# Order and size of the first weight loads, of the first two chunks' passes, and of ScalarE's splits ahead of three feed-forward stages

## What is computed

```
x += 0.5 * SwiGLU_1(rms(x))
x += Mixer_l(rms(x))        # layer 0: gated DeltaNet + short conv; layer 1: sliding-window attention
x += 0.5 * SwiGLU_2(rms(x)) # and a final RMSNorm after layer 1
SwiGLU(h) = (silu(h @ w_gate) * (h @ w_up)) @ w_down     # 1024 -> 2816 -> 1024
```

## Time and profile before

| | us |
|---|---|
| median of 3 executions | 996.03 (995.19 to 999.85) |
| profiled execution | 996.98 |
| its span, first to last instruction | 995.0 |
| TensorE busy in it | 978.2 |
| VectorE busy | 622.2 |
| ScalarE busy | 475.8 |

### The profile page before, as it was taken

The page is one execution under the profiler, slowest core; times in us unless marked ns, Lnnn a source line. Parts: engine busy times, 40 slices in busy tenths (PEclk is TensorE's granted clock), DMA queues, the critical chain, the costliest instruction groups (busy, mean ns, idle before and its releaser), DMA issues.

```text
span 995.0 us, 19436 instructions
## 1 busy us (share of the span) xinstructions
PE 978.2 (98%) x8172; PEld 959.3 (96%) x8172; DVE 622.2 (63%) x619; ACT 475.8 (48%) x527; POOL 78.4 (8%) x76
## 2 busy tenths in 40 slices
PE   8999999999999999999999999999999999999997
PEld 8999999999999999999999999999999998999996
DVE  6755555799955566555557655555789486555554
ACT  7644444656543454343436534343647365343443
POOL 0100101000000011010100110101002101000000
PEclk9999999999999999999999999999999999999999
DMA  9665656453433356656555565566551254656551
GB/s 293 223 230 183 206 174 211 130 172 122 135 120 96 117 170 214 209 174 206 183 197 170 177 203 186 194 195 216 165 174 48 81 184 158 225 191 193 190 190 42
DMA packets 136309, 172.84 MB, mean 174 GB/s; under 512 B 4309, under 2 KB 123850, under 8 KB 136266
## 3 DMA queue, kind: packets, MB, share of 16 engines
q1 hardware_dynamic: 135792, 171.63, 53.4%
q10 hardware_dynamic: 474, 0.58, 0.2%
HBM read 171.15 MB, written 1.05 MB: 173 GB/s over the span
## 4 chain that ended last, share of the span: by engine, by line
PE 90%; DVE 4%; ACT 2%; issue 2%; DMA 1%; POOL 0%; SPq 0%; POOLq 0%; ACTq 0%; DVEq 0%
PE bank L363 24%; PE bank L368 24%; PE bank L364 24%; PE bank L714 6%; PE bank L1525 3%; DVE w_lo L334 1%; DMA raw<-in_ffn_w_up 1%; ACT w_hi L322 1%; PE bank L954 1%; PE bank L941 1%; PE bank L1585 1%; DVE var L528 1%; PE bank L930 0%; POOL silu_r L691 0%; PE bank L1601 0%
## 5 line engine op out<-in xcount | busy, mean ns | idle before, releaser
L334 DVE TENSOR_TENSOR w_lo<-raw,w_hi 128x2048 fp32r<-128x2048 f32 x152 | 349.8, 2301 | 188.1 <-ACT w_hi L322 188.0
L363 PE MATMUL bank<-h_hi_rest,w_hi 128*128 128x256 f32 x1428 | 393.7, 278 | 0.7 <-DVE h_lo_rest L486 0.6
L364 PE MATMUL bank<-h_lo_rest,w_hi 128*128 128x256 f32 x1428 | 392.4, 277 | 0.0
L368 PE MATMUL bank<-h_hi_rest,w_lo 128*128 128x256 f32 x1428 | 385.0, 277 | 0.0
L322 ACT ACTIVATE w_hi<-raw 128x2048 fp32r<-128x2048 f32 x159 | 302.8, 1908 | 140.3 <-PE bank L368 138.5
L363 PEld LDWEIGHTS bank<-h_hi_rest,w_hi 128*128 128x128 f32 x1428 | 268.2, 188 | 1.4 <-DVE h_lo_rest L486 0.8
L364 PEld LDWEIGHTS bank<-h_lo_rest,w_hi 128*128 128x128 f32 x1428 | 268.2, 188 | 0.0
L368 PEld LDWEIGHTS bank<-h_hi_rest,w_lo 128*128 128x128 f32 x1428 | 263.9, 188 | 0.0
L363 PE MATMUL bank<-act_hi,w_hi 128*128 128x256 f32 x480 | 133.6, 278 | 3.8 <-DVE w_lo L334 3.8
L364 PE MATMUL bank<-act_lo,w_hi 128*128 128x256 f32 x480 | 133.4, 278 | 0.0
L368 PE MATMUL bank<-act_hi,w_lo 128*128 128x256 f32 x480 | 133.3, 278 | 0.0
(11 more groups left out here) (285 smaller groups left out, 1240.7 us busy)
## 6 DMA issues: line engine op xcount, KB each, us to landing
raw<-in_ffn_w_up SPq DMA_DIRECT2D x44, 1024.0 KB, 5.3
raw<-in_ffn_w_down SPq DMA_DIRECT2D x44, 1024.0 KB, 4.9
raw<-in_ffn_w_gate SPq DMA_DIRECT2D x43, 1024.0 KB, 5.3
raw<-in_hyb_w_in SPq DMA_DIRECT2D x14, 1024.0 KB, 5.4
raw<-in_swa_w_qkv SPq DMA_DIRECT2D x6, 1024.0 KB, 5.1
raw<-in_hyb_w_out SPq DMA_DIRECT2D x4, 1024.0 KB, 5.3
raw<-in_swa_w_o SPq DMA_DIRECT2D x4, 1024.0 KB, 5.1
raw<-in_ffn_w_gate SPq DMA_DIRECT2D x2, 512.0 KB, 6.9
```

The source lines that it names most:

```text
L334: nc.vector.tensor_tensor(w_lo[slot(ch)][:], raw[:, slot(ch), :], w_hi[slot(ch)][:].bitcast(F32), ALU.subtract).then_inc(lo_split, 1)
L363: nc.tensor.matmul(out_ap, w_hi[s][:, wcols], mv_hi, start=start, stop=False, skip_group_check=True)
L364: i = nc.tensor.matmul(out_ap, w_hi[s][:, wcols], mv_lo, start=False, stop=False, skip_group_check=True)
L368: return nc.tensor.matmul(out_ap, w_lo[s][:, wcols], mv_hi, start=False, stop=stop, skip_group_check=True)
```

## The change

Four edits. (1) The first chunk's weights come in DMAs of 256, 256 and 512 KB; ScalarE splits them after pairs 0, 1 and 2; TensorE does the high passes of row tiles 0 to 3, their low passes, the high passes of 4 to 7, their low passes. (2) The second chunk does the high passes of column tile 0, its low passes, then column tile 1 as before. (3) In every feed-forward stage the high half of c0+5 (`next_split((c0 + 2, 0))`) stands before `act_step(0)`; in those with n > 0 the high half of c0+4 stands before `norm_rstd`. (4) In the attention stage `turn_probs(1)` stands before `turn_q(3)`; ScalarE's order there is left as it is.

```
-        first_half_loaded = sem("first_half_loaded")
-        first_half_split = sem("first_half_split")
+        first_loaded = [sem("first_loaded0"), sem("first_loaded1")]
+        first_split_done = sem("first_split_done")
...
+        FIRST = [slice(0, 512), slice(512, 1024), slice(1024, 2048)]
+
+        def first_split(act_e, part):
+
+            act_e.wait_ge((*first_loaded, w_loaded[0])[part], 16)
+            cols = FIRST[part]
             nc.scalar.activation(w_hi[0][:, cols], raw[:, 0, cols], ACT.Copy) \
-              .then_inc((first_half_split, hi_split)[half], 1)
+              .then_inc(hi_split if part == 2 else first_split_done, 1)
...
-            dve.wait_ge((first_half_split, hi_split)[half], 1)
+            dve.wait_ge(*((hi_split, 1) if half else (first_split_done, 2)))
...
+            if ch[0] == 0:
+                for half in range(2):
+                    kts = range(half * KT // 2, (half + 1) * KT // 2)
+                    for kt in kts:
+                        if kt < KT // 2:
+                            pe.wait_ge(first_split_done, kt // 2 + 1)
+                        else:
+                            pe.wait_ge(hi_split, 1)
+                        pe.wait_ge(h_ready, kt // 2 + 1)
+                        for ft in range(HG):
+                            step(kt, ft, kt + ft == 0, False, 0)
+                    pe.wait_ge(*((lo_split, 1) if half else (first_lo_half, 1)))
+                    for ft in range(HG):
+                        for kt in kts:
+                            last = step(kt, ft, False, kt == KT - 1, 1)
+            elif ch[0] == 1:
+                pe.wait_ge(hi_split, 2)
                 for kt in range(KT):
+                    step(kt, 0, kt == 0, False, 0)
+                pe.wait_ge(*early)
+                for kt in range(KT):
+                    step(kt, 0, False, kt == KT - 1, 1)
+                pe.wait_ge(lo_split, 2)
+                for kt in range(KT):
+                    last = step(kt, 1, False, kt == KT - 1)
...
-                if j % 2:
-                    first_split(act_e, j // 2)
+                if j < 3:
+                    first_split(act_e, j)
...
-                for half, done in enumerate((first_half_loaded, w_loaded[0])):
-                    kts = slice(half * KT // 2, (half + 1) * KT // 2)
-                    sp.dma_start(raw[:, 0, half * 1024:(half + 1) * 1024].rearrange("p (a b) -> p a b", b=CW),
+                for cols, done in zip(FIRST, (*first_loaded, w_loaded[0])):
+                    kts = slice(cols.start // CW, cols.stop // CW)
+                    sp.dma_start(raw[:, 0, cols].rearrange("p (a b) -> p a b", b=CW),
                                  wg[:, kts, 0:CW]).then_inc(done, 16)
...
             gate_step(0)
+            next_split((c0 + 2, 0))
             act_step(0)
...
             gate_step(1)
-            next_split((c0 + 2, 0))
...
             values(0)
+            turn_probs(1)
             turn_q(3)
-            turn_probs(1)
             turn_o(0)
...
+                early = kind == "ffn" and n > 0
+                if early:
+                    split_hi(act_e, (c + 4, 0))
                 norm_rstd(act_e, n)
-                split_hi(act_e, (c + 4, 0))
+                if not early:
+                    split_hi(act_e, (c + 4, 0))
```

More of the change, by code:

```diff
@@ L322, in split_hi @@
             nc.scalar.activation(w_hi[slot(ch)][:], raw[:, slot(ch), :], ACT.Copy).then_inc(hi_split, 1)
-        def first_split(act_e, half):
-            act_e.wait_ge((first_half_loaded, w_loaded[0])[half], 16)
-            cols = slice(half * 1024, (half + 1) * 1024)
+        FIRST = [slice(0, 512), slice(512, 1024), slice(1024, 2048)]
+        def first_split(act_e, part):
+            act_e.wait_ge((*first_loaded, w_loaded[0])[part], 16)
+            cols = FIRST[part]
             nc.scalar.activation(w_hi[0][:, cols], raw[:, 0, cols], ACT.Copy) \
-              .then_inc((first_half_split, hi_split)[half], 1)
+              .then_inc(hi_split if part == 2 else first_split_done, 1)
         def split_lo(dve, ch):
@@ L377, in step @@
                                m_hi[kt], m_lo[kt], start=start, stop=stop, part=part)
-            if pairs_ready is not None:
-                first_chunk = number(ch) == 0
-                pe.wait_ge(*((first_half_split, 1) if first_chunk else (hi_split, number(ch) + 1)))
-                for kt in range(KT):
-                    if first_chunk and kt == KT // 2:
-                        pe.wait_ge(hi_split, 1)
+            if ch[0] == 0:
[15 more added lines that the diff above has]
+                pe.wait_ge(hi_split, 2)
+                for kt in range(KT):
+                    step(kt, 0, kt == 0, False, 0)
[5 more added lines that the diff above has]
+                    last = step(kt, 1, False, kt == KT - 1)
+            elif pairs_ready is not None:
+                pe.wait_ge(hi_split, number(ch) + 1)
+                for kt in range(KT):
                     if kt % 2 == 0:
@@ L388, in column_chunk @@
                         step(kt, ft, kt + ft == 0, False, 0)
+                pe.wait_ge(lo_split, number(ch) + 1)
                 for half in range(2):
[L390 to L393, removed]
                     for ft in range(HG):
```

## The result

The changed kernel takes 988.13 us (median of 4, 987.52 to 989.98) against 995.66 (median of 4, 995.19 to 999.85) for the kernel before; ratio 0.9917, 95% interval 0.9898 to 0.9937. So it is faster, as forecast, but by 7.5 us instead of 6.45. The profiled execution took 988.23, span 986.3, against 996.98 and 995.0: 8.75 us less. Some 2 us of gain are not in the prediction, and they are the question of the experiments.

What follows compares the result with a forecast made beforehand. TensorE, busy 978 of 995 us, was taken as the bound, so only its waits count. Gains of 6.2 and 0.9 less a loss of 0.65 made 6.45: 996.03 - 6.45 = 989.6 us, range 988.0 to 992.0.

Steps and rivals of the forecast that it cites:

- The three stalls: ffn1, ffn2, ffn3: TensorE's waits for c0+5's low half go wholly, 3 x 2.06 = 6.2 us gained.
- the product with up: Feed-forward chain: GpSimd's product would come 1.5 us after silu's end, at 364.75 in ffn1.
- The margin: Feed-forward stages: c0+5's low half would be done 2.4 us before TensorE wants it.
- The start: ffn0's first two chunks: smaller loads and reordered passes let c0+1 start at 15.5 instead of 16.43, 0.9 us gained.
- The cover argument at c0+5: ffn0: c0+5's earlier low half, 36.5 instead of 38.8, keeps a faster start from being partly given back there.
- The swap: Attention stage: q's copy comes onto the path, so `scores(3)` starts at 766.4 instead of 765.75, 0.65 us lost.
- the sum: Whole kernel: 6.2 + 0.9 - 0.65 = 6.45 us less, giving 989.6 us.
- rival E: First chunk: small waits drop TensorE's clock to 1.2 GHz, 5.7 us more per chunk, 1001.0 for two; chance 0.02.
- A: First chunk's loads: each extra load costs the queue time, c0+1 starts 0.9 late, 991.4 us; chance 0.07.
- B: Feed-forward stages: something else is late and half of each stall stays, 992.7 us; chance 0.08.
- C: Feed-forward stages: c0+4's early high half waits for its chunk, delays rstd, and the stalls stay, 995.8 us; chance 0.03.
- D: Attention stage: putting `turn_probs(1)` first costs nothing, 988.9 us; chance 0.05.

Runs made afterwards that it cites:

- ffn_only: Kernel before with only the high halves of c0+5 and c0+4 moved earlier in the feed-forward stages; 989.73 us against 997.22, ratio 0.9924.
- early4_only: Kernel before with only c0+4's high half moved ahead of `norm_rstd`; 992.26 us, ratio 0.9951.
- filled: Kernel before, stalls kept, with 15 extra unread matmuls before the wait for c0+5 in ffn1, ffn2, ffn3; 995.37 us, repeated 995.11; ratios 0.9993, 0.9986.
- held: Changed kernel, but TensorE also waits for w_lo of c0+6 before c0+5 in ffn1, ffn2, ffn3; 998.56 us, ratio to the kernel before 1.0023.
- start_only: Kernel before with only the first chunk's loads and passes and the second chunk's passes changed; 996.64 us, ratio 0.9998.
- swap_only: Kernel before with only `turn_probs(1)` put before `turn_q(3)` in the attention stage; 998.21 us, ratio 1.0014.

## Why the prediction was right, and where it was wrong

**The three stalls: right in mechanism and size.** 2.22, 2.2 (of 3.93) and 2.2 in position, so 6.6 instead of 6.2: the forecast stopped at the first matmul of c0+5 and left out that the second came late as well. `ffn_only`'s fastest execution is 6.1 below that of before. Within the chain one step was off: the product with up came 2.3 us after silu's end, not 1.5 (364.52 against 362.20). GpSimd's step lasted 2.16 us, since c0+4's low half on VectorE now ran beside it; the row of before had only a wait of VectorE to read it from. The margin was 1.6, not 2.4, so it cost nothing there, and it is what `early4_only` shows bare. c0+4's high half had 1.9 us of margin, not 3.4: its load landed 3.8 us before rstd, not 5.

**The start: right.** Forecast 0.9. In this pair 0.77; c0+1's start over the seven traces of each order has the means 16.41 and 15.45, so 1.0. The parts landed at 7.93, 8.76 and 10.28, as the queue's rate says (forecast 7.8, 8.6, 10.2); the splits stood at 8.21, 9.45 and 10.68. The first high halves of h were later than I had put them (7.49 against 6.84), but that place scatters from 6.23 to 7.71 over the traces of both orders. The cover argument at c0+5 was right in kind: without edit 3 there is a wait of 0.42, and the start's gain isn't measurable in the times.

**The swap: right in place, not seen whole in the total.** Forecast 0.65, measured 0.72 at `scores(3)`, and 0.26 (uncertainty 0.2) between the lowest steps.

**A small gain not forecast:** 0.28 to 0.35 within ffn0 and hyb. In the kernel before, the matmuls of ffn0's c0+5, whose weights came just in time, stand 0.118 apart, in the changed one 0.114, which is 0.25 of it. Cause not tried.

**What failed** is the sum: the sentence under rival E that the clock "nor did it fall in the 1.9 us stalls". It had fallen behind ffn2's stall, in the very trace I read; I had looked at windows around ffn1's only. The end of that paragraph, that the trace shows no pause that brought the low clock back, is wrong for the same reason. The term that is missing from the sum is the half-clock stretch that a stall brings with some probability, 1.7 us each. From the fastest executions the work is worth 7.05, and the positions add up to the same: 6.6 + 0.8 + 0.35 - 0.7. That is 0.6 above the forecast of 6.45, mostly from the restarts and the small gain above. The medians differ by 8.9, so about 1.8 is the clock's. That TensorE's idleness in the stalls is a cause, and not position or pace, is shown from both sides: filling the stalls brings the steps down without moving the work, and idle waits put back bring them up. `filled` also sizes it: its means are 0.9 and 1.5 below those of the kernel before beside it (995.76 and 996.65; 995.41 and 996.95). The rest of the 1.8 may be hyb's: six of the sixteen traces have a half-clock stretch there (`held` among them, but none of the changed kernel's own), and there the last idle wait lies 48 us before it. Of the executions of kernels without stalls 17 of 44 lie above their lowest step where edit 1 or 2 is missing, and 5 of 25 where both are in; that hints at the start, but is too little to show it, and it was not tried by itself. Rival E had the mechanism and the wrong sign: the change takes idleness away, so the clock could only pay for it. And I took the 0.95 by which the profiled execution lay above the median for noise, where it was part of a step.

Rivals A, B, C and D did not happen: landings follow the rate, no stall is left, rstd isn't delayed, and the swap does cost.

Open: what brings on hyb's stretch, and why in four of the sixteen traces TensorE's pace between 785 and 797 us is 0.118 us a matmul instead of 0.114.

## What to carry to other kernels

An idle wait of the bounding engine may cost more than its length: after each, look at the granted clock and the spacing of the following matmuls, in every place where the stall repeats, and look at the spread of the executions, for steps. When two moves both work on one stall, price each alone: here one moved line gave all that the two gave together. And an edit that starts the bound engine earlier pays only if what was just in time later on is moved as well.

## What the runs showed of the hardware that I had not expected

TensorE's granted clock went from 2.4 to 1.2 GHz right behind an idle wait of 1.92 us (before, ffn2) and of 2.43 us (`held`, ffn3), though TensorE had been busy without a gap ahead of it and was again behind it. It did not do so behind the equal waits in the other two stages of the same executions: over the traces of `before`, `start_only` and `swap_only` it was one of nine such waits, in `held` one of three. And it fell in hyb, at 298 to 300 us in six traces, with TensorE busy at 1.00 and without a wait since 250. The Trainium skill ("TensorE: Matmul & The Clock Gate", HAM oscillation — how this bites in real kernels) describes kernels in which waits for a DMA, of some 3 to 5 us, bring the low clock back again and again; the traces agree in kind, with shorter waits.

GpSimd waits for VectorE. Its 128x512 multiplication lasts 1.29 to 1.31 us when no low half of VectorE (which reads two operands from SBUF) runs beside it. When it starts 0.2, 0.75, 1.01 or 1.45 us before the end of such a low half, it lasts 1.36, 1.92, 2.16 or 2.60, and so ends 1.15 to 1.17 after it each time (363.28 and 364.43 in ffn1 of the changed kernel). The Trainium skill ("SBUF — State Buffer", Terms) has this as a shared pair of ports that one engine holds for a whole instruction; the trace agrees.
